# First unit of a two-layer transformer kernel: another order of weight quarters, normed tiles and squares, and the rotary angles computed later

## The chip, the core and the metric

The kernel runs on one core of a Trainium2 chip. Its metric is device time in microseconds (us). The engines meant below are TensorE (PE in the profile, its weight loads PEld), VectorE (DVE), ScalarE (ACT), GpSimd (POOL) and SyncE (SP), which issues the weight loads. Each engine works through its own list of instructions in order; they are tied together by semaphores (`wait_ge`, `then_inc`) that are written by hand.

## The reference

512 tokens of width 1024 go through two layers. Each layer is a feed-forward block, a mixing block (differential attention with rotary angles on queries and keys, beside a gated branch), cross attention to 256 memory rows, and a second feed-forward block:

```
def swiglu(x, wgu, wd):
    gate, up = jnp.split(x @ wgu, 2, axis=-1)
    return (jax.nn.silu(gate) * up) @ wd
cos, sin = rope_tables(positions)
for i in range(2):
    h = h + 0.5 * swiglu(rms_norm(h, ffn1_norm[i]), ffn1_wgu[i], ffn1_wd[i])
    hn = rms_norm(h, mix_norm[i])
    q, k, v, gu, gv = jnp.split(hn @ w_in[i], ...)
    q, k = partial_rope(q, cos, sin), partial_rope(k, cos, sin)
    h = h + concat([diff_attention(q, k, v), gated(gelu(gu), layer_norm(gelu(gv)))]) @ w_out[i]
    h = h + cross_attention(rms_norm(h, ...), rms_norm(mem, ...), ...)
    h = h + 0.5 * swiglu(rms_norm(h, ffn2_norm[i]), ffn2_wgu[i], ffn2_wd[i])
return rms_norm(h, final_norm)
```

## The kernel before

Every product is made of three matmuls of rounded halves: hi by hi, hi by lo, lo by hi. The high half of a weight or an activation is a rounded copy that ScalarE writes (`w_hi`, `hn_hi`); the low half is the difference, which VectorE writes (`w_lo`, `hn_lo`). Weights come in units of 128 x 2048 elements (1 MB) into two slots of `raw`, unit by unit; SyncE issues the loads of a slot once `w_split` says that the low half of the unit two before is done. For each unit, ScalarE rounds (L692), VectorE subtracts (`split_unit`, L1221), TensorE multiplies. A unit of the gate and up weights is 48 matmuls of 512 columns: eight slices k of the contraction, for each a gate and an up product.

The activations are not normed before the product. `hn` is h times the gain; the inverse root mean square of each token is multiplied in afterwards. For the very first block it comes from squares of the input (ScalarE, `square_input`, one instruction for each tile of 128 tokens, each waiting for the one before, L718), a scaling on VectorE (L1297), a power on GpSimd (L603), and four transposes on TensorE that spread it over the partitions (`send_rb`, L2074). ScalarE copies that out as `rb` (L707), and the gating of the first unit starts there.

**The start.** The input comes in four tiles of 128 tokens. TensorE transposes them (L2096) into eight banks; VectorE copies the first six of them to `h`, ScalarE the last two (`copy_input`, L724). The first unit's weights come in four quarters: quarter n has slices 2n and 2n + 1, in two DMAs of 128 KB each (L509). ScalarE writes hi parts in this order: squares of tile 0, the two copies, normed slices 0 and 1, weight quarter 0, slices 2 and 3, quarter 1, slices 4 and 5, squares 1, quarters 2 and 3, slices 6 and 7, squares 2 and 3, then the whole of unit 1. TensorE does the hi products of slices 0 to 3, then their lo-weight products, then waits for the whole low half of the unit (L1292) before slices 4 to 7. After unit 0 it sends `rb`, then starts unit 1.

VectorE, behind the low halves of unit 1, computes the rotary angles (`angles()`, 15 small instructions in a chain, L1310 to L1324) and only then gates unit 0 (L1377).

**The mixing block** starts with the projections GV, QQ, KK, GU, VV, of two units each (48 matmuls a unit, L2053 to L2055). VectorE here splits the two units of QQ, takes statistics of the gated branch (L1767 to L1774), splits the first unit of KK, waits for the inverse deviations that GpSimd raises to a power (L646, `rstd`), norms four tiles with them (L1781 to L1785), writes their low halves (L1789), scales the memory rows (L1795), and then splits the second unit of KK (L1221 again). ScalarE's `late_setup()` takes the sines of the angles after it has rounded the first unit of KK; queries are rotated after the second unit of KK is split.

Of the kernel before, what the change touches and what calls it, by code (L numbers as in the profile page):

```python
# [7 lines left out]
P = 128  # L8
# [5 lines left out]
KT = D // P  # L14
ST = S // P
# [93 lines left out]
def macaron_kernel(nc, x, mem, positions, ffn1_norm, ffn1_wgu, ffn1_wd, mix_norm, w_in,  # L109
# [7 lines left out]
    ACT = mybir.ActivationFunctionType  # L117
# [4 lines left out]
    with ctx:  # L122
        def sem(name):
            return ctx.enter_context(nc.semaphore(name))
# [157 lines left out]
        first_loaded = [sem(f"first_loaded{n}") for n in range(4)]  # L282
        half_split = sem("half_split")
        x_squared = sem("x_squared")
        w_rounded = sem("w_rounded")
        w_split = sem("w_split")
        w_used = sem("w_used")
# [382 lines left out]
        def _(act):  # L670
# [15 lines left out]
            def round_unit(L, u, i=0, per=2):  # L686

                n = unit_no(L, u, i, per)
                s = u % 2
                act.wait_ge(w_loaded[s], 32 * (L * (UNITS // 2) + u // 2 + (per // 2) * i + 1))  # L690
                act.wait_ge(w_used, n + 1)
                act.activation(w_hi[:, s, :], raw[:, s, :], ACT.Copy).then_inc(w_rounded, 1)  # L692

            def round_tile(no, m, gcol):

                act.wait_ge(h_ready, no)
                act.activation(hn_hi[:, slice(m, m + 1), :], h[:, slice(m, m + 1), :], ACT.Copy,
                               scale=gains[:, slice(gcol, gcol + 1)]).then_inc(hn_rounded, 1)
# [10 lines left out]
            def first_unit(n):  # L709
                act.wait_ge(first_loaded[n], 32)  # L710
                act.activation(unit_quarter(w_hi, n), unit_quarter(raw, n), ACT.Copy)\
                   .then_inc((half_rounded, half_rounded, half_rounded, w_rounded)[n], 1)

            def square_input(t):
                act.wait_ge(x_loaded[t], 16)
                if t:
                    act.wait_ge(x_squared, t)
                act.activation(tmp[:, 0:2, :], x_in[:, t, :].rearrange("p (a c) -> p a c", c=S), ACT.Square,  # L718
                               accum_out=xsq[:, t:t + 1]).then_inc(x_squared, 1)

            def copy_input(n):
                t, c = divmod(n, 2)
                act.wait_ge(x_turned, n + 1)
                act.activation(h[:, 4 * c:4 * c + 4, t * P:(t + 1) * P],  # L724
                               ps[:, n % 6, :].rearrange("p (k c) -> p k c", c=P), ACT.Copy).then_inc(h_ready, 1)

            square_input(0)
            copy_input(2 * ST - 2)
            copy_input(2 * ST - 1)
            act.wait_ge(setup_dve, HALF + 1)  # L730
            round_tile(KT, 0, 0)
            round_tile(KT, 1, 1)
            first_unit(0)
            round_tile(KT, 2, 2)
            round_tile(KT, 3, 3)
            first_unit(1)
            round_tile(KT, 4, 4)
            round_tile(KT, 5, 5)
            square_input(1)
            first_unit(2)  # L740
            first_unit(3)
            round_tile(KT, 6, 6)
            round_tile(KT, 7, 7)
            square_input(2)
            square_input(3)
            round_unit(0, 1)
            def late_setup():
                act.wait_ge(lam_sums_ready, 1)
                act.activation(lam_s[:, :, :], lam_s[:, :, :], ACT.Exp).then_inc(setup_act, 1)
                act.wait_ge(angles_ready, 1)  # L750
                for c in range(2):
                    for n in range(2):
                        act.activation(rope[:, :, c, n * HALF:(n + 1) * HALF], ang[:, 2 - c, :, :], ACT.Sin)\
                           .then_inc(setup_act, 1)
# [460 lines left out]
        def _(dve):  # L1215
# [26 lines left out]
            def low_tile(no, m, gcol):  # L1242
                dve.wait_ge(hn_rounded, no)
                dve.scalar_tensor_tensor(out=hn_lo[:, slice(m, m + 1), :], in0=h[:, slice(m, m + 1), :],
                                         scalar=gains[:, slice(gcol, gcol + 1)],
                                         in1=hn_hi[:, slice(m, m + 1), :].bitcast(f32),
                                         op0=ALU.mult, op1=ALU.subtract).then_inc(hn_ready, 1)
# [21 lines left out]
            for n in range(2 * ST - 2):  # L1269
                t, c = divmod(n, 2)  # L1270
                if n == 2:
                    dve.wait_ge(setup_pe, 1)
                    dve.tensor_copy(gains[:, 0:LAYERS * KT], ps[:, 7, 0:LAYERS * KT]).then_inc(setup_dve, 1)
                dve.wait_ge(x_turned, n + 1)
                dve.tensor_copy(h[:, 4 * c:4 * c + 4, t * P:(t + 1) * P],
                                ps[:, n % 6, :].rearrange("p (k c) -> p k c", c=P)).then_inc(h_ready, 1)
            done[0] += 1
            low_tile(1, 0, 0)
            low_tile(2, 1, 1)
# [8 lines left out]
            setup(dve.tensor_copy(gains[:, LAYERS * KT:], ps[:, 6, LAYERS * KT:90]))  # L1288
            low_tile(5, 4, 4)
            low_tile(6, 5, 5)  # L1290
            dve.wait_ge(w_rounded, 1)
            dve.tensor_tensor(out=unit_half(w_lo, 1), in0=unit_half(raw, 1), in1=unit_half(w_hi, 1).bitcast(f32),  # L1292
                              op=ALU.subtract).then_inc(w_split, 1)
            low_tile(7, 6, 6)
            low_tile(8, 7, 7)
            dve.wait_ge(x_squared, ST)
            dve.tensor_scalar(msq[:, :], xsq[:, :], 1.0 / D, EPS, ALU.mult, ALU.add).then_inc(ms_ready, 1)  # L1297
            dve.wait_ge(setup_pe, 3)
# [4 lines left out]
                                        in0=lam_in[:, 2 * n, :].rearrange("p (l d) -> p l d", d=64),  # L1303
                                        in1=lam_in[:, 2 * n + 1, :].rearrange("p (l d) -> p l d", d=64), op=ALU.mult))
            dve.tensor_reduce(lam_s[:, :, :], lam_pr[:, :, :, :], AX.X, ALU.add).then_inc(lam_sums_ready, 1)
            split_unit(0, 1)

            def angles():
                for t in range(ST):
# [8 lines left out]
                for c in (c1, c2, c3):  # L1318
# [4 lines left out]
                setup(dve.tensor_tensor(out=ang[:, 2, :, :], in0=ang[:, 2, :, :], in1=ang[:, 1, :, :], op=ALU.max))  # L1323
                dve.tensor_scalar(ang[:, 2, :, :], ang[:, 2, :, :], -1.0, math.pi / 2, ALU.mult, ALU.add)\  # L1324
                   .then_inc(angles_ready, 1)

            angles()

            def head_gains():
                for l in range(LAYERS):  # L1330
# [418 lines left out]
            for L in range(0, LAYERS):  # L1749
# [10 lines left out]
                split_unit(L, QQ)  # L1760
                mean_square(L * 4 + 2, 7)
                split_unit(L, QQ + 1)
                dve.wait_ge(small_loaded, L * 64 + 64)
                for t in range(ST):
                    dve.wait_ge(gelu_ready, L * 4 + t + 1)
# [284 lines left out]
        def _(pe):  # L2050
# [58 lines left out]
            def ffn(L, f, up, stage):  # L2109
# [5 lines left out]
                def wait_split(kind, i):  # L2115
                    pe.wait_ge(w_split, base + FFN_AT[kind, i] + 3)

                def whole_unit(i, hook=None, waits=False):
                    in_halves = start_of_all and i == 0
                    if in_halves:  # L2120
                        for k in range(4):
                            if k % 2 == 0:
                                pe.wait_ge(half_rounded, k // 2 + 1)
                            pe.wait_ge(hn_ready, hn_no(L, stage, k))
                            for g in range(2):
                                a = g * 1024 + k * P
                                pe.matmul(ps[:, g, :], w_hi[:, 0, a:a + P], hn_hi[:, k, :], start=k == 0, stop=False)
                                pe.matmul(ps[:, g, :], w_hi[:, 0, a:a + P], hn_lo[:, k, :], start=False, stop=False)
                        pe.wait_ge(half_split, 1)
                        for k in range(4):  # L2130
                            for g in range(2):
                                a = g * 1024 + k * P
                                pe.matmul(ps[:, g, :], w_lo[:, 0, a:a + P], hn_hi[:, k, :], start=False, stop=False)
                        pe.wait_ge(setup_dve, HALF + 2)
                        pe.transpose(ps[:, 7, LAYERS * KT:LAYERS * KT + ST], pos_f[:, :], ident[0:ST, 0:ST])\
                          .then_inc(setup_pe, 1)
                    else:
                        wait_split("N", i)
                    for k in range(4 if in_halves else 0, KT):
                        if waits:  # L2140
                            pe.wait_ge(hn_ready, hn_no(L, stage, k))
                        if hook and k in hook:
                            hook[k]()
                        if in_halves and k == 4:
                            wait_split("N", i)
                        for g in range(2):
                            a = g * 1024 + k * P
                            last = product(ps[:, 2 * i + g, :], w_hi[:, i % 2, a:a + P], w_lo[:, i % 2, a:a + P],
                                           hn_hi[:, k, :], hn_lo[:, k, :], k == 0, k == KT - 1)
                    last.then_inc(w_used, 1)  # L2150
# [257 lines left out]
                    token_sums((L * STAGES + stage) * 9, 6)  # L2408

                whole_unit(0, None, True)  # L2410
                if start_of_all:
                    send_rb()
                if not start_of_all:
                    sum_tokens()
                whole_unit(1, None if start_of_all else {4: send_rb}, True)
                whole_unit(2)
                third_unit()
                first_chunk()
# [366 lines left out]
```

## Time and profile before

| | |
|---|---|
| median of 3 runs | 2084.46 us (2083.52 to 2085.33) |
| the profiled execution | 2084.04 us |
| its span | 2082.2 us, 1.8 us less than its time |
| granted TensorE clock | 0.999 over the span |
| DMA | 212.35 MB, 102 GB/s on the mean |

The span is what the profile's clock runs over, from the first instruction to the last. All times "at" a point below count from its start. A line of a timeline gives start, length, engine, source line, operation, what is written and read, and in brackets the idle time ahead of it with what ended it. Where several like instructions follow each other, they are one line with their count, and the length is that of all.

### The profile page before, as it was taken

To read this page: it belongs to the slowest core of one execution; us is meant where nothing else is said; L and a number is where in the kernel's file an instruction comes from. 1 tells how busy PE (TensorE), PEld (TensorE's weight loads), DVE (VectorE), ACT (ScalarE), POOL (GpSimd) and SP (SyncE) were. 2 spreads that over 40 slices of the span, in tenths; PEclk is the share of its full clock that TensorE was granted. 3 is DMA by queue.
4 is the path that set the end of the run, shared out by engine and by line. 5 is a ranking of instruction groups with operands and counts; after the bars stand their busy time and mean duration, and the time that the engine had idled before them with its cause. 6 is when DMAs were issued, how large, how long until landed. Compare 5 with 4: busy or idle time off the path is not lost.

```text
span 2082.2 us, 35834 instructions
## 1 busy us (share of the span) xinstructions
PE 2068.2 (99%) x14719; PEld 1918.0 (92%) x14719; DVE 1654.0 (79%) x2476; ACT 984.8 (47%) x1491; POOL 151.0 (7%) x120
## 2 busy tenths in 40 slices
PE   9999999999999999999999999999999999999998
PEld 7999998889888889999989999988898888999998
DVE  7998886659754789898799988766696458898886
ACT  6444444446533544444464444443564345454443
POOL 0000003100120300000110000030002102000002
PEclk9999999999999999999999999999999999999999
DMA  6333323323331343333233333143233214333321
GB/s 198 102 112 104 101 86 116 122 81 102 101 103 41 91 127 112 115 104 92 72 121 112 112 107 112 59 149 102 68 116 101 81 61 132 102 112 92 112 87 57
DMA packets 268031, 212.35 MB, mean 102 GB/s; under 512 B 7422, under 2 KB 234332, under 8 KB 267868
## 3 DMA queue, kind: packets, MB, share of 16 engines
q1 hardware_dynamic: 264608, 205.55, 31.7%
q10 hardware_dynamic: 3260, 4.51, 0.7%
q8 instruction: 117, 1.92, 0.4%
q14 instruction: 46, 0.38, 0.1%
HBM read 207.93 MB, written 2.10 MB: 101 GB/s over the span
## 4 chain that ended last, share of the span: by engine, by line
PE 92%; DVE 5%; ACT 2%; issue 1%; DMA 0%; POOL 0%; SPq 0%; DVEq 0%; ACTq 0%; POOLq 0%
PE ps L2180 18%; PE ps L2053 13%; PE ps L2055 13%; PE ps L2054 13%; PE ps L2360 11%; PE ps L2361 11%; PE ps L2362 11%; DVE nb L1909 1%; DVE w_lo L1231 1%; ACT ex L1120 1%; DVE ex L1929 1%; DVE ps L1907 0%; PE ps L2514 0%; PE ps L2705 0%; DMA x_in<-in_x_dram 0%
## 5 line engine op out<-in xcount | busy, mean ns | idle before, releaser
L2180 PE MATMUL ps<-hid_hi,wn_hi 128*128 128x256 f32 x1088 | 211.9, 276 | 0.0
L2180 PE MATMUL ps<-hid_lo,wn_hi 128*128 128x256 f32 x1088 | 211.9, 276 | 0.0
L2180 PE MATMUL ps<-hid_hi,wn_lo 128*128 128x256 f32 x1088 | 211.8, 276 | 0.0
L1490 DVE SCALAR_TENSOR_TENSOR h<-ps,h 128x512 f32<-128x512 f32 x224 | 152.6, 683 | 30.4 <-PE ps L2180 26.8
L692 ACT ACTIVATE w_hi<-raw 128x2048 fp32r<-128x2048 f32 x61 | 117.0, 1918 | 123.1 <-PE ps L2055 90.8
L2180 PEld LDWEIGHTS ps<-hid_lo,wn_hi 128*128 128x128 f32 x1088 | 163.8, 188 | 0.0
L2180 PEld LDWEIGHTS ps<-hid_hi,wn_hi 128*128 128x128 f32 x1088 | 163.8, 188 | 0.0
L2180 PEld LDWEIGHTS ps<-hid_hi,wn_lo 128*128 128x128 f32 x1088 | 163.7, 188 | 0.0
L2360 PE MATMUL ps<-hn_hi,form_hi 128*128 128x256 f32 x576 | 159.0, 276 | 0.0
L2362 PE MATMUL ps<-hn_hi,form_lo 128*128 128x256 f32 x576 | 159.0, 276 | 0.0
L2361 PE MATMUL ps<-hn_lo,form_hi 128*128 128x256 f32 x576 | 159.0, 276 | 0.0
L2360 PE MATMUL ps<-t_hi,form_hi 128*128 128x256 f32 x576 | 159.0, 276 | 0.0
L2361 PE MATMUL ps<-t_lo,form_hi 128*128 128x256 f32 x576 | 159.0, 276 | 0.0
L2362 PE MATMUL ps<-t_hi,form_lo 128*128 128x256 f32 x576 | 159.0, 276 | 0.0
L2360 PE MATMUL ps<-t_hi,more_hi 128*128 128x256 f32 x576 | 159.0, 276 | 0.0
L2361 PE MATMUL ps<-t_lo,more_hi 128*128 128x256 f32 x576 | 159.0, 276 | 0.0
L2362 PE MATMUL ps<-t_hi,more_lo 128*128 128x256 f32 x576 | 159.0, 276 | 0.0
L1221 DVE TENSOR_TENSOR w_lo<-raw,w_hi 128x2048 fp32r<-128x2048 f32 x49 | 114.3, 2332 | 48.6 <-ACT w_hi L692 48.3
L2053 PE MATMUL ps<-hn_hi,w_hi 128*128 128x512 f32 x376 | 147.8, 393 | 0.7 <-DVE w_lo L1292 0.5
L2055 PE MATMUL ps<-hn_hi,w_lo 128*128 128x512 f32 x376 | 146.5, 390 | 0.0
L2054 PE MATMUL ps<-hn_lo,w_hi 128*128 128x512 f32 x376 | 146.4, 389 | 0.0
L598 POOL TENSOR_TENSOR sumsq<-sumsq,tmp 128x512 f32<-128x512 f32 x56 | 102.0, 1821 | 340.4 <-ACT tmp L703 335.5
(356 smaller groups left out, 6161.8 us busy)
## 6 DMA issues: line engine op xcount, KB each, us to landing
sraw<-in_ffn_wgu_dram SPq DMA_DIRECT2D x144, 512.0 KB, 4.9
raw<-in_ffn_wd_dram SPq DMA_DIRECT2D x48, 512.0 KB, 3.8
raw<-in_ffn_wd_dram SPq DMA_DIRECT2D x80, 256.0 KB, 4.0
raw<-in_w_in_dram SPq DMA_DIRECT2D x40, 512.0 KB, 4.5
raw<-in_cross_wkv_dram SPq DMA_DIRECT2D x32, 512.0 KB, 4.2
raw<-in_ffn_wgu_dram SPq DMA_DIRECT2D x30, 512.0 KB, 4.8
raw<-in_w_out_dram SPq DMA_DIRECT2D x16, 512.0 KB, 4.3
raw<-in_cross_wq_dram SPq DMA_DIRECT2D x16, 512.0 KB, 3.9
```

The lines of the kernel that those rows point to most:

```text
L598: pool.tensor_tensor(out=sumsq[:, :], in0=sumsq[:, :], in1=tmp[:, m2, :], op=ALU.add)\
L692: act.activation(w_hi[:, s, :], raw[:, s, :], ACT.Copy).then_inc(w_rounded, 1)
L1120: last = act.activation(ex[:, b, br, 0:N], ps[:, 4 + 2 * b + br, 0:N], ACT.Exp, bias=nb[:, b, br:br + 1], accum_out=sm[:, b, br:br + 1])
L1221: dve.tensor_tensor(out=w_lo[:, s, 0:z], in0=raw[:, s, 0:z], in1=w_hi[:, s, 0:z].bitcast(f32), op=ALU.subtract).then_inc(w_split, 1)
L1490: dve.scalar_tensor_tensor(out=h[:, m, :], in0=ps[:, down_bank(c, m), :], scalar=0.5, in1=h[:, m, :], op0=ALU.mult, op1=ALU.add).then_inc( ...
L2053: pe.matmul(dst, a_hi, b_hi, start=start, stop=False)
L2054: pe.matmul(dst, a_hi, b_lo, start=False, stop=False)
L2055: return pe.matmul(dst, a_lo, b_hi, start=False, stop=stop)
L2180: last = pe.matmul(ps[:, bank, c], w, src[:, b, c], start=opens, stop=stop and n == 2, skip_group_check=half == 1)
L2360: pe.matmul(dst, a_hi, b_hi, start=start and k == 0, stop=False, skip_group_check=not start)
L2361: pe.matmul(dst, a_hi, b_lo, start=False, stop=False, skip_group_check=not start)
L2362: last = pe.matmul(dst, a_lo, b_hi, start=False, stop=k == 3, skip_group_check=not start)
```

## The change

ScalarE's order at the start becomes: squares 0, the copy of the seventh bank only (under a semaphore of its own, `last_left`), slice 0, quarter 0, slices 1 and 2, quarter 1, slices 3 and 4, quarter 2, slice 5, quarter 3, slices 6 and 7, unit 1, and then squares 1 to 3. The eighth bank is copied by VectorE. Slices 0 to 3 no longer wait for it.

TensorE does the hi products of slices 4 to 7 as soon as the weights are rounded, and their lo-weight products last. `send_rb` moves from the front of unit 1 to between its slices 1 and 2. VectorE splits unit 1 ahead of the mean squares and the small set-up work. `angles()` moves into the mixing block of layer 0, between the split of the second unit of QQ and the statistics.

```
 ScalarE
             square_input(0)
-            copy_input(2 * ST - 2)
-            copy_input(2 * ST - 1)
+            copy_last_left()
             act.wait_ge(setup_dve, HALF + 1)
-            round_tile(KT, 0, 0)
-            round_tile(KT, 1, 1)
+            act.wait_ge(last_left, 1)
+            round_tile(KT - 2, 0, 0)
             first_unit(0)
-            round_tile(KT, 2, 2)
-            round_tile(KT, 3, 3)
+            round_tile(KT - 2, 1, 1)
+            round_tile(KT - 2, 2, 2)
             first_unit(1)
+            round_tile(KT - 2, 3, 3)
             round_tile(KT, 4, 4)
+            first_unit(2)
             round_tile(KT, 5, 5)
-            square_input(1)
-            first_unit(2)
             first_unit(3)
             round_tile(KT, 6, 6)
             round_tile(KT, 7, 7)
-            square_input(2)
-            square_input(3)
             round_unit(0, 1)
+            for t in range(1, ST):
+                square_input(t)
 VectorE
+            dve.wait_ge(x_turned, 2 * ST)
+            dve.tensor_copy(h[:, 4:8, (ST - 1) * P:ST * P],
+                            ps[:, (2 * ST - 1) % 6, :]...).then_inc(h_ready, 2)
...
+            low_tile(7, 6, 6)
+            low_tile(8, 7, 7)
             dve.wait_ge(w_rounded, 1)
             dve.tensor_tensor(out=unit_half(w_lo, 1), ...).then_inc(w_split, 1)
-            low_tile(7, 6, 6)
-            low_tile(8, 7, 7)
+            split_unit(0, 1)
             dve.wait_ge(x_squared, ST)
...
-            split_unit(0, 1)
...
-            angles()
...
                 split_unit(L, QQ + 1)
+                if L == 0:
+                    angles()
 TensorE, unit 0, behind the products of slices 0 to 3
+                        pe.wait_ge(w_rounded, 1)
+                        for k in range(4, KT):   # w_hi by hn_hi and w_hi by hn_lo
...
                         wait_split("N", i)
+                        for k in range(4, KT):   # w_lo by hn_hi
...
-                if start_of_all:
-                    send_rb()
-                whole_unit(1, None if start_of_all else {4: send_rb}, True)
+                whole_unit(1, {2 if start_of_all else 4: send_rb}, True)
```

## Rows read from the trace of the kernel before

**Rows 1.** The page, part 1: engine, busy us, share of span, instructions.
```profile
PE 2068.2 (99%) x14719; PEld 1918.0 (92%) x14719; DVE 1654.0 (79%) x2476; ACT 984.8 (47%) x1491; POOL 151.0 (7%) x120
```
**Rows 2.** Waits of TensorE: us in total, times, longest us.
```profile
PE ps L2127 <- ACT w_hi L711: 0.9, 1, 0.9
PE ps L2053 <- DVE w_lo L1292: 0.5, 1, 0.5
```
**Rows 3.** Timeline of ScalarE at the start.
```profile
9.31 1.09 ACT L724 ACTIVATE h<-ps 128x512 f32<-128x512 f32 x2
10.50 1.33 ACT L697 ACTIVATE hn_hi<-h,gains 128x512 fp32r<-128x512 f32 x2
11.74 0.61 ACT L711 ACTIVATE w_hi<-raw 128x512 fp32r<-128x512 f32 x1
...
19.77 1.06 ACT L718 ACTIVATE tmp<-x_in 128x1024 f32<-128x1024 f32 x1
20.83 1.90 ACT L692 ACTIVATE w_hi<-raw 128x2048 fp32r<-128x2048 f32 x1
```
**Rows 4.** Second and tenth weight DMA: issue (timeline), landing (DMA view, us from issue).
```profile
3.44 0.49 SPq L509 DMA_DIRECT2D raw<-in_ffn_wgu_dram  x1
raw<-in_ffn_wgu_dram SPq DMA_DIRECT2D x1, 128.0 KB, 7.8
...
9.78 3.52 SPq L500 DMA_DIRECT2D raw<-in_ffn_wgu_dram  x1
raw<-in_ffn_wgu_dram SPq DMA_DIRECT2D x1, 512.0 KB, 9.5
```
**Rows 5.** Timelines of VectorE and GpSimd at the start.
```profile
11.25 1.41 DVE L1244 SCALAR_TENSOR_TENSOR hn_lo<-h,gains,hn_hi 128x512 fp32r<-128x512 f32 x2 [1.69 <-ACT hn_hi L697]
...
22.76 2.29 DVE L1221 TENSOR_TENSOR w_lo<-raw,w_hi 128x2048 fp32r<-128x2048 f32 x1 [0.43 <-ACT w_hi L692]
...
21.21 1.02 POOL L603 TENSOR_TENSOR rtok<-msq,m_half 128x4 f32<-128x4 f32 x1 [19.19 <-DVE msq L1297]
```
**Rows 6.** Timeline of TensorE at the start.
```profile
12.40 0.50 PE L2127 MATMUL ps<-hn_hi,w_hi 128*128 128x512 f32 x1 [0.86 <-ACT w_hi L711]
...
24.34 0.60 PE L2074 MATMUL ps<-ident,rtok 128*128 128x128 f32 x4
...
25.11 0.50 PE L2053 MATMUL ps<-hn_hi,w_hi 128*128 128x512 f32 x1 [0.17 <-DVE w_lo L1221]
```
**Rows 7.** Timeline of VectorE: first of the angles, and what follows the last.
```profile
24.97 1.02 DVE L1310 TENSOR_SCALAR ang<-invf,pos_t 128x8 f32<-128x8 f32 x4
...
28.10 0.68 DVE L1377 TENSOR_TENSOR Gn<-ps,rb 128x512 f32<-128x512 f32 x1
```
**Rows 8.** Timelines of TensorE, GpSimd and VectorE in layer 0's mixing block.
```profile
394.09 0.39 PE L2053 MATMUL ps<-w_hi,hn_hi 128*128 128x512 f32 x1
404.97 0.39 PE L2053 MATMUL ps<-w_hi,hn_hi 128*128 128x512 f32 x1
...
382.49 2.90 POOL L646 TENSOR_TENSOR rstd<-vareps,m_half 128x16 f32<-128x16 f32 x1 [4.95 <-DVE vareps L1774]
...
385.42 2.29 DVE L1221 TENSOR_TENSOR w_lo<-raw,w_hi 128x2048 fp32r<-128x2048 f32 x1 [2.94 <-ACT w_hi L692]
387.62 1.11 DVE L1781 TENSOR_SCALAR k_tok<-k_tok,mv,rstd 128x128 f32<-128x128 f32 x4
...
401.28 2.28 DVE L1221 TENSOR_TENSOR w_lo<-raw,w_hi 128x2048 fp32r<-128x2048 f32 x1
```
**Rows 9.** Timelines of VectorE and GpSimd later in layer 0: a power beside a subtraction.
```profile
716.78 1.22 DVE L1358 TENSOR_TENSOR t_lo<-t_raw,t_hi 128x1024 fp32r<-128x1024 f32 x1
716.95 1.93 POOL L603 TENSOR_TENSOR rtok<-msq,m_half 128x4 f32<-128x4 f32 x1 [3.13 <-DVE msq L1251]
```
**Rows 10.** Timelines of VectorE and TensorE: first tile of the blocked stage.
```profile
72.32 0.42 DVE L1402 TENSOR_TENSOR G<-ps,G 128x256 f32<-128x256 f32 x1 [0.41 <-ACT G L835]
...
73.06 0.28 PE L2360 MATMUL ps<-t_hi,form_hi 128*128 128x256 f32 x1
```

More of the change, by code:

```diff
@@ L284, in macaron_kernel @@
         x_squared = sem("x_squared")
+        last_left = sem("last_left")
         w_rounded = sem("w_rounded")
@@ L719, in square_input, with copy_last_left @@
                                accum_out=xsq[:, t:t + 1]).then_inc(x_squared, 1)
-            def copy_input(n):
-                t, c = divmod(n, 2)
+            def copy_last_left():
+                n = 2 * ST - 2
                 act.wait_ge(x_turned, n + 1)
-                act.activation(h[:, 4 * c:4 * c + 4, t * P:(t + 1) * P],
-                               ps[:, n % 6, :].rearrange("p (k c) -> p k c", c=P), ACT.Copy).then_inc(h_ready, 1)
+                act.activation(h[:, 0:4, (ST - 1) * P:ST * P], ps[:, n % 6, :].rearrange("p (k c) -> p k c", c=P), ACT.Copy)\
+                   .then_inc(last_left, 1)
             square_input(0)
-            copy_input(2 * ST - 2)
-            copy_input(2 * ST - 1)
+            copy_last_left()
             act.wait_ge(setup_dve, HALF + 1)
-            round_tile(KT, 0, 0)
-            round_tile(KT, 1, 1)
+            act.wait_ge(last_left, 1)
+            round_tile(KT - 2, 0, 0)
             first_unit(0)
-            round_tile(KT, 2, 2)
-            round_tile(KT, 3, 3)
+            round_tile(KT - 2, 1, 1)
+            round_tile(KT - 2, 2, 2)
             first_unit(1)
+            round_tile(KT - 2, 3, 3)
             round_tile(KT, 4, 4)
+            first_unit(2)
             round_tile(KT, 5, 5)
-            square_input(1)
-            first_unit(2)
             first_unit(3)
@@ L1276, in _ @@
                                 ps[:, n % 6, :].rearrange("p (k c) -> p k c", c=P)).then_inc(h_ready, 1)
+            dve.wait_ge(x_turned, 2 * ST)
+            dve.tensor_copy(h[:, 4:8, (ST - 1) * P:ST * P],
+                            ps[:, (2 * ST - 1) % 6, :].rearrange("p (k c) -> p k c", c=P)).then_inc(h_ready, 2)
             done[0] += 1
@@ L2136, in whole_unit @@
                           .then_inc(setup_pe, 1)
-                    else:
-                        wait_split("N", i)
-                    for k in range(4 if in_halves else 0, KT):
+                        pe.wait_ge(w_rounded, 1)
+                        for k in range(4, KT):
+                            pe.wait_ge(hn_ready, hn_no(L, stage, k))
+                            for g in range(2):
+                                a = g * 1024 + k * P
+                                pe.matmul(ps[:, g, :], w_hi[:, 0, a:a + P], hn_hi[:, k, :], start=False, stop=False)
+                                pe.matmul(ps[:, g, :], w_hi[:, 0, a:a + P], hn_lo[:, k, :], start=False, stop=False)
+                        wait_split("N", i)
+                        for k in range(4, KT):
+                            for g in range(2):
+                                a = g * 1024 + k * P
+                                last = pe.matmul(ps[:, g, :], w_lo[:, 0, a:a + P], hn_hi[:, k, :],
+                                                 start=False, stop=k == KT - 1)
+                        last.then_inc(w_used, 1)
+                        return
+                    wait_split("N", i)
+                    for k in range(KT):
                         if waits:
@@ L2143, in whole_unit @@
                             hook[k]()
-                        if in_halves and k == 4:
-                            wait_split("N", i)
                         for g in range(2):
```

## Prediction

> **What bounds the kernel now.** I read the page's busy shares first: TensorE is busy for 99% of the span, VectorE for 79%, ScalarE for 47% [rows 1]. So time can come only from TensorE's idle stretches, and none of its work is removed. Next the waits of TensorE: at the start two long ones are named, 0.9 us for the first rounded weights and 0.5 us for the second low half [rows 2]. Then the timelines: the real work starts at 12.40 and unit 1 at 25.11, with four transposes between the units [rows 6]. Later TensorE meets hardly a wait; what counts there is how much room each low half has, which the timeline shows and the table of waits does not.
>
> **The start, step by step.** A unit of 48 matmuls takes 404.97 - 394.09 = 10.88 us [rows 8], 0.227 each.
>
> *ScalarE.* Two copies took 1.09, so one takes about 0.55 and ends at 9.86. The normed slice then starts at 9.96 instead of 10.50 and takes about 0.62 (10.50 to 11.74 for two) [rows 3]. Quarter 0 would be next at 10.6, but its second DMA, issued at 3.44, lands 7.8 later, at 11.24 [rows 4]. Rounding it (0.61) ends at 11.89, where before it ended at 12.35: TensorE starts 0.45 earlier, not the 1.1 that the order alone would give. Slices and quarters follow, 0.52 to 0.62 each, the last slice ends near 18.3. Unit 1 can't be rounded before its second load lands, at 9.78 + 9.5 = 19.28 [rows 4]; 1.90 for it gives 21.2, where before it ended at 22.73 [rows 3]. The three squares, 1.22 apart as each waits for the one before, start near 21.1, 22.3, 23.5. Before, the last square started at 19.77 and the power ended at 21.21 + 1.02 = 22.23, 2.46 later [rows 3, 5]; so it now ends at 26.0.
>
> *VectorE.* The eighth copy fits into its idle 1.69 [rows 5] and costs nothing; if that cover were gone, 0.6. A low slice takes 0.7. The low half of slices 0 and 1 is late now: slice 1 is rounded behind quarter 0 and is ready at 13.25. Slice 3 follows at 15.0, half of the first low weights (half of 2.29, about 1.2) at 16.2, the other slices at 0.7 each until 19.2, the second half at 20.3. Unit 1 is split from 21.2 to 23.5, where before it ended at 25.05 [rows 5].
>
> *TensorE.* From 11.93: 48 matmuls (10.88), 0.1 for one small transpose, 0.4 of waiting for slice 1, 0.1 for the half, 0.2 for two restarts. Sum 23.6; unit 1 starts there, just behind its low half at 23.5. Slices 0 and 1 of it (12 matmuls) end at 26.35, the power has ended at 26.0, so the spreading transposes don't wait. They take 0.65. Unit 1 therefore ends 25.11 - (23.65 + 0.65) = 0.8 earlier than before.
>
> *What the head start keeps.* `rb` arrives some 2.1 later than before (27.05 for 24.94 [rows 6]). The angles, 28.10 - 24.97 = 3.13 us [rows 7], no longer stand ahead of the first gating, so this starts at 27.7 instead of 28.10; but the table load for the silu, behind `rb` on ScalarE, makes the silu some 0.15 late, and with it the loads and VectorE's work up to the blocked stage. There VectorE waited 0.41 for ScalarE and gave `G` at 72.74, 0.3 ahead of TensorE at 73.06 [rows 10]. With TensorE 0.8 early and VectorE's queue 0.15 late, that `G` comes at 72.4 against 72.26: 0.2 of the head start goes. I take -0.6, with -0.9 and +0.2 as ends (the lower if nothing of it is lost, the upper if the wait for slice 1 and the late queue cost 0.4 each more).
>
> **The angles in their new place.** They are 3.13 us of VectorE [rows 7] in front of the statistics. Behind them in its queue stand the statistics, the split of KK's first unit, the norming, the memory rows and the split of KK's second unit, for which TensorE comes at 404.97. This split ended at 401.28 + 2.28 = 403.56: 1.4 of room [rows 8].
>
> First the plain count. The power for `rstd` started at 382.49 and took 2.90 [rows 8], then VectorE still waited for ScalarE and split KK's first unit; norming started at 387.62. Shifted by 3.13 the power would run 385.62 to 388.52, norming would start at 388.6, 1.0 late, and 0.4 of the room would be left. Cost nothing.
>
> But the shift puts the power beside the split. The split needs `w_hi` (ready at 385.4) and follows the statistics at once, at about 385.5; the power starts 0.1 behind it. The trace has the same constellation: a subtraction from SBUF started at 716.78 and took 1.22, a power started at 716.95, and took 1.93 [rows 9], where a power of the same shape otherwise takes 1.02 [rows 5]. It ended 0.88 behind the end of the subtraction, as if 0.14 of it had run before and the rest had waited; the subtraction was not longer. So here: the split ends at 385.52 + 2.29 = 387.8, the power 2.90 - 0.14 later, at 390.6; norming starts at 390.6, 3.0 late, and the split of KK's second unit runs 404.3 to 406.6. TensorE waits 1.6, and a restart costs 0.1 more: +1.7. The ends are 0 (the plain count) and +2.2 (a power stretched in the ratio 1.93 to 1.02 takes 5.5 and ends at 391.1).
>
> The Trainium skill, "SBUF — State Buffer", section "Who interferes with whom", says that a VectorE instruction with two SBUF inputs and a GpSimd instruction that reads SBUF exclude each other for their whole length, and that the one which comes second stands still. By that rule the sum is +1.7 whichever of the two is first, since both must have run before the norming; by the ratio it would be +2.2. The row agrees with the rule (end of the subtraction plus 0.88), but shows it only for a power of 4 elements, not of 16.
>
> The next split in VectorE's queue is that of GU, which TensorE needs a whole unit (10.88) later, so nothing of the delay is passed on; without that cover up to 3.0 would come again. ScalarE's sines wait for angles that are done before the statistics, and so before 385.4, when ScalarE asks. Layer 1 has no angles and isn't changed.
>
> **Sum.** -0.6 + 1.7 = +1.1 us on the profiled execution's 2084.04, which is 0.4 below the median shown. On the median: 2084.46 + 1.1 = 2085.5.
>
> **Rivals.**
>
> A. The power isn't held up, or holds up little: the room of 1.4 covers the plain 1.0. Only the start counts: -0.6, 2083.9. For it: rows 9 show another shape, and the order at 385.5 hangs on 0.1 us. Against it: in either order the two would have to run side by side.
>
> B. Slower on the other side of my sum: unit 1's load decides the squares. Rounding of unit 1 now stands ahead of three squares and has no room behind the landing at 19.28, where it had 1.5 before (20.83) [rows 3, 4]. The place is `send_rb` in the middle of unit 1, the price is each microsecond that the power ends later than 26.35, and it decides from a landing 0.4 later than in this trace. With a landing 1.9 later it costs 1.5, beside 1.7 in the mixing block and hardly any gain kept: +2.8, 2087.2. For it: single loads here take between 7.8 and 9.5 to land. Against it: the loads are issued as before, so they should land as before.
>
> C. The start does what its order promises, the stall is as forecast, and the sum is near zero: gain 1.1 or more if landings come earlier, 2084.8. It is inside the range.
>
> A bigger gain is excluded: all waits of TensorE at the start are below 2 us together [rows 2, 6].
>
> **Chances.** Forecast 0.6, A 0.2, B 0.1, C 0.1. What a measurement of this kernel can tell from no change is 0.2%, 4.2 us, and all four cases lie within it; outside of it I leave 0.02 for faster and 0.04 for slower (an unseen stall that comes back in each blocked stage). The range, 2083.1 to 2087.0, holds A, the forecast and C with half a microsecond of scatter, and most of B.
>
> **What would show it.** TensorE's first matmul of unit 0 at 11.9 and of unit 1 at 23.6; unit 1 rounded from 19.3; the first power ended at 26.0 and no wait before the spreading transposes; a wait of 0.2 for `G` near 72.3. In the mixing block, L646 of layer 0 some 5.0 long instead of 2.90 and a wait of TensorE for L1221 of 1.6 near 404, while layer 1 keeps 2.90 and no wait. If L646 is 2.90 and the wait is missing, A is right; if TensorE waits ahead of L2074, B.

## The result, and the profile after

| | time, median | executions | ratio to before |
|---|---|---|---|
| before | 2084.39 us (2083.44 to 2085.49) | 20 | |
| after | 2087.69 us (2085.80 to 2090.83) | 20 | 1.0017, 95% interval 1.0011 to 1.0024 |

The changed kernel is 3.3 us slower, three times the forecast's +1.1 and 0.7 above the upper end of the range. It stays within the 0.2% that was named as the bound of "same". Its executions also scatter twice as much: 5.0 us from lowest to highest, against 2.05. The profiled execution took 2087.64 (span 2085.9), 3.60 above that of before.

The same line of the page's part 1 as in [rows 1]: TensorE is busy 2.4 us longer, though it does no more matmuls.

```profile
PE 2070.6 (99%) x14719; PEld 1919.2 (92%) x14719; DVE 1655.8 (79%) x2477; ACT 984.4 (47%) x1490; POOL 152.7 (7%) x120
```

The waits of TensorE. The two of [rows 2] are gone, a wait for the low half of the second unit of key weights (KK) is new:

```profile
PE ps L2056 <- DVE w_lo L1221: 1.9, 1, 1.9
...
PE ps L2099 <- DMA x_in<-in_x_dram: 0.6, 1, 0.6
PE ps L2195 <- issue: 0.3, 1, 0.3
```

**Where the time came from.** I compared the start of TensorE's nth matmul in both traces (14719 in each); the difference, after minus before, is called the shift here. It reads -0.35 at 30 us, once `rb` is sent, +0.33 at 75 us, +0.45 from 80 to 404 us, +4.19 at 412 us, +3.68 at the end. So the head start is small, it is lost with the first blocked tile, and 3.74 us come in at one place of the mixing block.

*The start*: ScalarE (answers to [rows 3]), then the spreading transposes, `G`'s product on VectorE and TensorE behind it (to [rows 6, 10]).

```profile
16.21 0.63 ACT L712 ACTIVATE w_hi<-raw 128x512 fp32r<-128x512 f32 x1 [1.30 <-DMA raw<-in_ffn_wgu_dram]
19.98 1.92 ACT L693 ACTIVATE w_hi<-raw 128x2048 fp32r<-128x2048 f32 x1 [0.78 <-DMA raw<-in_ffn_wgu_dram]
24.27 1.06 ACT L719 ACTIVATE tmp<-x_in 128x1024 f32<-128x1024 f32 x1
27.77 0.60 ACT L708 ACTIVATE rb<-ps 128x512 f32<-128x512 f32 x1 [2.35 <-PE ps L2077]
28.39 1.28 ACT L784 ACT_TABLE_LOAD   x1
29.68 0.63 ACT L784 ACTIVATE Gn<-Gn 128x512 f32<-128x512 f32 x1
...
27.14 0.60 PE L2077 MATMUL ps<-ident,rtok 128*128 128x128 f32 x4
...
72.79 0.41 DVE L1403 TENSOR_TENSOR G<-ps,G 128x256 f32<-128x256 f32 x1
...
73.31 0.36 PE L2375 MATMUL ps<-t_hi,form_hi 128*128 128x256 f32 x1
```

ScalarE now waits for two loads where the old order had room. TensorE's first product is a different matter: it did not wait for weights in this execution. The first quarter was rounded at 11.94. Ahead of the product stand 16 transposes of the identity whose results nobody reads (`keep_busy`), behind the turning of the last input tile, and these ended at 12.24. Three rows of after, then that of before, where they ended at 11.54:

```profile
11.32 0.62 ACT L712 ACTIVATE w_hi<-raw 128x512 fp32r<-128x512 f32 x1
...
10.33 1.91 PE L2084 MATMUL ps<-ident 128*128 128x128 f32 x16
12.35 0.47 PE L2130 MATMUL ps<-hn_hi,w_hi 128*128 128x512 f32 x1
...
9.63 1.91 PE L2081 MATMUL ps<-ident 128*128 128x128 f32 x16
```

The spreading transposes at 27.14 did not wait for the power, but the silu stands behind `rb` (27.77 to 28.37) and the table load: it starts at 29.68. Its row of before:

```profile
28.82 0.63 ACT L784 ACTIVATE Gn<-Gn 128x512 f32<-128x512 f32 x1 [1.94 <-DVE Gn L1377]
```

So it is 0.86 late, where 0.15 was forecast. `G` at 72.79 is 0.47 later than in [rows 10] (0.86 less the 0.41 for which VectorE had waited there).

*The mixing block* (answers to [rows 7] and [rows 8]): VectorE and GpSimd, and the first product that waited.

```profile
377.40 1.41 DVE L1313 TENSOR_SCALAR ang<-invf,pos_t 128x8 f32<-128x8 f32 x4
...
386.35 2.29 DVE L1221 TENSOR_TENSOR w_lo<-raw,w_hi 128x2048 fp32r<-128x2048 f32 x1
...
386.46 4.93 POOL L647 TENSOR_TENSOR rstd<-vareps,m_half 128x16 f32<-128x16 f32 x1 [8.48 <-DVE vareps L1777]
...
405.09 2.28 DVE L1221 TENSOR_TENSOR w_lo<-raw,w_hi 128x2048 fp32r<-128x2048 f32 x1
...
407.43 0.50 PE L2056 MATMUL ps<-w_hi,hn_hi 128*128 128x512 f32 x1 [1.85 <-DVE w_lo L1221]
```

The angles run from 377.40 to 380.92, 3.52 and not 3.13 us. The power is 4.93 long beside the split (forecast 5.0), and the split for which TensorE waits ends at 407.37 (forecast 406.6).

*The clock.* What no step of the prediction had stands in the stretches behind the wait. Columns: stretch, its length, busy time of each engine, then the granted clock of TensorE (1.00 is its level of 2.4 GHz, 0.50 that of 1.2 GHz), DMA share and GB/s.

```profile
405.00:407.50 2.50, 0.65 (x4) 0.23 (x2) 2.50 (x4) 2.50 (x4) 0.00 (x0) 1.00 0.00 0
409.00:412.00 3.00, 3.00 (x8) 2.32 (x8) 2.83 (x10) 0.00 (x0) 0.00 (x0) 0.50 0.96 327
```

The first stretch holds the idle time; in the second TensorE is never idle, yet eight matmuls fall into it where an execution at full clock has fifteen (e9, below). Three of them:

```profile
409.14 0.63 PE L2056 MATMUL ps<-w_hi,hn_hi 128*128 128x512 f32 x1
409.57 0.63 PE L2057 MATMUL ps<-w_lo,hn_hi 128*128 128x512 f32 x1
410.00 0.63 PE L2058 MATMUL ps<-w_hi,hn_lo 128*128 128x512 f32 x1
```

They are 0.43 apart instead of 0.227. Of the 3.74 that come in, 2.02 are there at the first product behind the wait, 1.72 come behind it.

### The profile page after: what moved, and what is told of

Same layout as the page of the kernel before. It is cut to its first block, busy times and chain, and to the rows that moved or that the text cites. A ratio compares the mean times of both kernels' runs of the same rounds, so it can differ in the third digit from the quotient of the medians.

```text
span 2085.9 us, 35836 instructions
## 1 busy us (share of the span) xinstructions
PE 2070.6 (99%) x14719; PEld 1919.2 (92%) x14719; DVE 1655.8 (79%) x2477; ACT 984.4 (47%) x1490; POOL 152.7 (7%) x120
## 4 chain that ended last, share of the span: by engine, by line
PE 91%; DVE 6%; ACT 1%; issue 1%; DMA 0%; SPq 0%; POOL 0%; DVEq 0%; ACTq 0%; POOLq 0%
PE ps L2195 18%; PE ps L2056 13%; PE ps L2058 13%; PE ps L2057 13%; PE ps L2375 11%; PE ps L2376 11%; PE ps L2377 11%; DVE nb L1912 1%; DVE w_lo L1231 1%; ACT ex L1120 1%; DVE ex L1932 1%; DMA raw<-in_ffn_wgu_dram 0%; DVE ps L1910 0%; PE ps L2718 0%; PE ps L2527 0%
```

## The experiments

Theory at the outset: the angles stall TensorE in the mixing block by 2 us and the clock falls behind the stall (+1.6 in some executions); the start gains nothing, because `rb`, and behind it VectorE, is late. Rival: the start, through its landings, makes the excess and the scatter. The kernel before was run on the same chip as each group. A ratio's 95% interval is about 1.9 us to either side in all of these groups, so among kernels that lie 1 to 2 us apart the traces decide, not the medians.

**Each half alone** (before: 2084.37, 33 executions).

```
e1: the kernel before, angles() moved ahead of layer 0's statistics
e2: the changed kernel, angles() back at their old place
```

> The kernel before with one edit: the angles stand behind the split of QQ's second unit, the start stays as it was. Theory M (the slowdown sits in the mixing block: the power is held up by the split, TensorE waits about 2.0 us for KK's second unit, and the granted clock then halves for about 3.4 us, which costs about 1.7 more): +3.3 to +3.9 us, L647's counterpart near 4.9 long, one wait of 1.8 to 2.0 for the split, one stretch at half clock. Rival S (the new order of the start costs the time, the angles add only the wait): +1.7 to +2.0, and the rest is missing here.

Measured: 2086.21 (2085.83 to 2088.22), ratio 1.0011 (1.0002 to 1.0019). In its profile the start's shift is -0.14, TensorE waits 1.9 for `w_lo`, and the shift goes from -0.11 to +3.68, with the half clock in it. The median, +1.8, is what the rival expected and misses the theory's +3.3; the profiled execution, +3.1, comes near the theory. So the wait came as forecast, but the fall of the clock is no fixed part of it.

> The changed kernel with the angles back in their old place, behind the small set-up work and ahead of the first gating. Theory M: no wait in the mixing block and no stretch at half clock there; what is left is the start: the power is 4 us later than before, the angles push the first gating to about 30, and TensorE loses about 1.4 us at the first blocked tile, so +0.5 to +1.5. Rival S: +1.5 to +2 or more, with the loss spread over the start.

Measured: 2084.68 (2084.37 to 2086.12), ratio 1.0003 (0.9994 to 1.0012); no wait for `w_lo`. Its first product came at 11.61, its head start is -1.09 at 30 us, and +0.93 at 150 us: 2 us go in the first blocked stage, as here the angles too stand ahead of the first gating.

**Three ways round the stall** (e3 and e4 on the chip of e1; e5 on that of e9).

```
e3: angles() behind mss, ahead of the split of KK's first unit
e4: KK's second unit does its 32 products with w_hi first, then those with w_lo
```

> The changed kernel with the angles two instructions further back in VectorE's queue: behind the variances and the mean squares of the memory, ahead of the split of KK's first unit, so beside the power, where VectorE waited 2.9 us for ScalarE. Theory M: the power takes 2.9 to 3.3, norming starts no more than 0.5 late, no wait for KK's second unit, clock full: +0.4 (the start alone), within -0.3 and +1. Rival P (any VectorE work beside the power holds it up): the power takes over 4, but as the split no longer stands behind both, at most 1 us is lost and the 1.4 of room covers it: the same time, told apart only by the length of L647. Rival S: +1.5 to +2.

Measured: 2084.68 (2083.91 to 2086.83), ratio 1.0003 (0.9995 to 1.0012). The angles fill VectorE's idle time beside the power, which is back at its old length:

```profile
383.18 1.03 DVE L1313 TENSOR_SCALAR ang<-invf,pos_t 128x8 f32<-128x8 f32 x4
...
386.31 2.28 DVE L1221 TENSOR_TENSOR w_lo<-raw,w_hi 128x2048 fp32r<-128x2048 f32 x1
388.52 1.11 DVE L1784 TENSOR_SCALAR k_tok<-k_tok,mv,rstd 128x128 f32<-128x128 f32 x4
...
383.29 2.90 POOL L647 TENSOR_TENSOR rstd<-vareps,m_half 128x16 f32<-128x16 f32 x1 [4.95 <-DVE vareps L1775]
```

> The changed kernel with its angles where they are; only TensorE's second unit of KK is reordered: its 32 products with the rounded weights run first and wait only for ScalarE's rounding, its 16 products with the low weights last, behind the wait for the split. Theory M: the power still takes 4.9 and VectorE is just as late, but TensorE has 7.3 us of work in front of that wait: no idle time, full clock, +0.4 (within -0.3 and +1). If VectorE's lateness costs in another place too, +1 to +2 and a wait behind KK.

Measured: 2085.04 (2083.69 to 2085.54), ratio 1.0003 (0.9994 to 1.0012). The power stays long, but TensorE has work until `w_lo` is there; no wait, clock full:

```profile
387.47 4.94 POOL L647 TENSOR_TENSOR rstd<-vareps,m_half 128x16 f32<-128x16 f32 x1 [8.47 <-DVE vareps L1777]
```

They stand 0.3 and 0.7 above the kernel before. The changed kernel itself was not run in this group; in three others it stands 3.3, 4.2 and 3.7 above. The stall with what follows it is most of the loss, and two different edits that take it away show it.

```
e5: in layer 0 split_unit(L, KK) behind the first norm tile, so that nothing
    runs beside the power
```

> The changed kernel with the split of KK's first unit of layer 0 behind the norming of the first tile instead of ahead of it, so that VectorE stands still beside the power. If the split holds the power up, L647 takes 2.90 again in layer 0 and norming starts 2.0 earlier, but the split's 2.2 comes out of it again ahead of KK's second unit: the wait there stays about 2.0 and the time +2.3 to +4. If the power is slow for another reason (the time at which it runs), it takes 4.9 here too and the wait grows to 4.

One profiled execution, 2086.30 (before on this chip 2083.95): the power is 2.90 again, and TensorE waits no less.

```profile
386.20 2.90 POOL L647 TENSOR_TENSOR rstd<-vareps,m_half 128x16 f32<-128x16 f32 x1 [8.48 <-DVE vareps L1777]
...
391.62 2.29 DVE L1221 TENSOR_TENSOR w_lo<-raw,w_hi 128x2048 fp32r<-128x2048 f32 x1
...
404.99 2.29 DVE L1221 TENSOR_TENSOR w_lo<-raw,w_hi 128x2048 fp32r<-128x2048 f32 x1
...
407.34 0.50 PE L2059 MATMUL ps<-w_hi,hn_hi 128*128 128x512 f32 x1 [2.03 <-DVE w_lo L1221]
```

The stretched power is therefore no loss of its own: power and split have to run one after the other between the statistics and the rest of the norming, in whichever order. What costs is 3.5 us of VectorE ahead of both, while VectorE stands idle beside the power.

**Is it the idle time that makes the clock fall?** (before: 2083.95, 27 executions.)

```
e9: the changed kernel again
e6: the changed kernel, and ahead of KK's second unit in layer 0
    for _ in range(8): pe.matmul(ps[:, bank, :], nil[:, :], hn_hi[:, 0, :], ...)
```

> The changed kernel itself again, as the measure for the next one on the same chip. Start +0.3 to +0.7 (from the runs with the angles elsewhere), wait for KK's second unit +2.0, and in a part of the executions +1.7 for a stretch at half clock: each time lies near 2086.8 or near 2088.5, the median between, +2.4 to +4.1. If the clock has nothing to do with it, the times lie in one group.

Measured: 2088.13 (2086.37 to 2090.57), ratio 1.0019 (1.0010 to 1.0028). The eleven times don't fall into two groups; they are spread over the whole range, so the clock is not all that scatters. In its profile the same wait of 1.9 leaves the clock full:

```profile
409.00:412.00 3.00, 3.00 (x15) 2.49 (x14) 2.76 (x15) 0.00 (x0) 0.00 (x0) 1.00 0.84 264
```

> The changed kernel, with 8 matmuls of 512 columns put in front of TensorE's wait for KK's second unit in layer 0; their stationary tile is all zeros and they add nothing to the sums. They take 1.8 of the 2.0 us of idle time. If idle time is what brings the clock down, it stays full in every execution and the time is that of the wait and the start alone, +2.3 to +2.7, with no second group above: 0.5 to 1.5 below the changed kernel's median. If the clock falls for another reason, or the wait alone is the cost, it is no faster than the changed kernel, +3.3.

Measured: 2087.41 (2085.52 to 2088.24), ratio 1.0016 (1.0007 to 1.0025). The filler takes the place of the wait, to the tenth of a microsecond:

```profile
405.80 1.97 PE L2468 MATMUL ps<-hn_hi,nil 128*128 128x512 f32 x8
407.82 0.50 PE L2059 MATMUL ps<-w_hi,hn_hi 128*128 128x512 f32 x1
```

The median falls by 0.7 and the spread from 4.2 to 2.7 us; all 11 executions have a mean clock of 0.999 or 1.000, where 4 of 11 of e9 have 0.998. This speaks for the theory, weakly: the median missed the +2.3 to +2.7 that were expected, and a listed 0.998 is no sure sign of a fall behind a wait. The kernel before has it in 5 of 33 executions on each of two chips and in none of 27 here. And 3.5 us stay with no listed drop in them.

**Does the start keep its gain if `rb` comes earlier?**

```
e8: e3, and square 1 ahead of the third quarter, square 2 ahead of unit 1,
    send_rb at step 1 of unit 1 instead of 2
e7: the same with the angles where the change has them
```

> The changed kernel with the angles beside the power (as in the earlier run), squares 1 ahead of weight quarter 2 and squares 2 ahead of unit 1, where ScalarE waited 1.3 and 0.8 us for loads, and the spreading transposes between slices 0 and 1 of unit 1. The power then ends about 1.5 earlier, `rb` and the first gating with it, and VectorE is no longer late at the first blocked tile: the head start of 0.2 to 1.1 at unit 2 isn't lost there, so 0.8 below the kernel with the angles beside the power and -0.3 to -0.8 against before. If the head start goes in another place, +0.3 as with the angles moved alone.

Measured (chip of e9): 2083.74 (2082.84 to 2084.76), ratio 0.9998 (0.9989 to 1.0007). The shift is +0.25 at 30 us and still +0.25 at 150 us: nothing is lost in the blocked tiles. The silu starts 0.11 later than before, on TensorE that is 0.25 late, and VectorE waits for ScalarE again ahead of `G`:

```profile
28.93 0.63 ACT L785 ACTIVATE Gn<-Gn 128x512 f32<-128x512 f32 x1
...
72.57 0.42 DVE L1404 TENSOR_TENSOR G<-ps,G 128x256 f32<-128x256 f32 x1 [0.45 <-ACT G L836]
```

It is the lowest of all versions, 0.2 below the kernel before where 0.3 to 0.8 were expected, and cannot be told from it.

**Do the parts add up?** By the medians so far, 0.3 (e2) and 1.8 (e1) stand against 3.3 to 4.2. So all were run side by side (before: 2085.50, 33 executions), e10 as e2, e11 as e1, e12 the changed kernel.

> The changed kernel with the angles back behind the second feed-forward block, as in e2 (first unit new, angles old), beside e11 and e12 on one chip. Parts that add up: the first unit's new order is worth the same wherever it stands, +0.3 to +1.5 against the kernel before on this chip, and its profile has a shift at 80 us between 0 and 1.5 (in the seven profiles with the new first unit so far: 0.05 to 1.47, mean 0.76), set by when the weight quarters and unit 1's weights land. Rival (the two parts make each other worse): +0.3 here as before, and the changed kernel more than 1.0 above this one and e11 taken together. A clock below 0.999 in about one execution in ten, as in the kernel before (5 of 33, 0 of 27).

> The kernel before with the angles alone moved, as in e1. Expected +1.8 to +2.4: the stall of 2.0 at the first product with w_lo of the key unit, and in some executions the clock at half for some microseconds behind it (those have a mean clock of 0.998 and stand 1.3 to 2.5 above the others). Its start is that of the kernel before, so its full-clock executions should spread no more than 1.5 us.

> The changed kernel once more, on the chip of e10 and e11. Parts that add up: its difference from the kernel before is that of e10 plus that of e11 within 0.7, with the spread of both (4 us from lowest to highest). Parts that make each other worse: more than 1.0 above the sum (batches one and two, on two chips, gave 0.3 + 1.8 against 3.3 to 4.2). If executions with clock 0.998 are left out, the drop goes and what is left over the sum is the first unit's alone.

> The changed kernel with squares 1 and 2 back in ScalarE's gaps (square 1 before the third weight quarter's rounding, square 2 before unit 1's) and the spreading of rms one step earlier; the angles where the change has them. Stall as in the changed kernel (2.0). If what is lost at the start is ScalarE's three squares standing behind unit 1's rounding, and through them VectorE late in the first blocked tile, this is 0.6 to 1.2 below e12. If it is the landing of the quarters, which no order of the squares changes, it is within 0.3 of e12.

| kernel | median | range | over before |
|---|---|---|---|
| e10, start alone | 2085.52 | 2084.59 to 2087.89 | 0.0 |
| e11, angles alone | 2087.06 | 2086.57 to 2089.11 | +1.6 |
| e12, changed | 2089.20 | 2087.19 to 2091.37 | +3.7 |
| e7, changed, `rb` earlier | 2088.19 | 2085.42 to 2090.17 | +2.7 |

The ratios are 1.0000 (0.9992 to 1.0009), 1.0011 (1.0002 to 1.0020), 1.0017 (1.0008 to 1.0026) and 1.0011 (1.0002 to 1.0020). The parts do not add up by their medians, 1.6 against 3.7, and both fell short of what was expected of them (+0.3 and +1.8 at the least). e7's median is 1.0 lower than e12's, and its shift is 1.18 at 30 us and 1.18 at 150 us, where e12 goes from 1.03 to 1.93. The traces show that this 0.9 is the late `rb`; the medians agree, but could not show it alone. e11, with the old start, had a shift of 1.64 at 30 us: there the weights came late under the old order too (ScalarE waited 0.8 for the first quarter, TensorE's first product came at 13.85).

**More executions of the changed kernel in profile**, e13 to e15, and one of e6, e16 (before, one execution: 2083.64).

> The changed kernel, one profiled execution more. (a) The clock falls behind the wait for w_lo: matmuls at 0.43 apart for some 3 us, +1.6 there, start shift at 80 us 0 to 1. (b) Clock full, start shift above 1. (c) The wait above 2.3. Seen so far in three executions: wait 1.9 in each, clock fallen in one, start shift 0.45, 1.01 and 1.53.

> As e13. If (a), two or three of the executions e13 to e15 have the clock at half behind the wait; if the chance is that of the angles alone (3 of 22 executions with a mean clock of 0.998), none or one.

> As e13. The executed time of each of the three is, by the terms read so far, that of the kernel before on this chip plus 0.0 to 1.2 of the start, 2.0 of the wait and 0 or 1.6 of the clock; a time more than 0.5 above the terms read in its own trace would mean a fourth cause.

> The changed kernel with eight matmuls that add zeros ahead of the wait, one execution more. Clock full throughout; wait and filler together 2.0 to 2.2 by the first product behind them. If its shift over the kernel before is above 2.8 at the end, it must be the start's (b), since neither (a) nor a longer idle is left.

The six profiled executions of the changed kernel. The second column is the time less that of before on its chip (the median; for e13 to e15 the one execution); the others are read from the shifts.

| execution | over before | shift at 30 us | at 150 us | added at the first product behind the wait | added behind it |
|---|---|---|---|---|---|
| after | +3.25 | -0.35 | +0.45 | 2.02 | 1.72 |
| e9 | +3.55 | +0.40 | +1.38 | 2.02 | 0.12 |
| e12 | +2.66 | +1.03 | +1.93 | 2.03 | 0.14 |
| e13 | +4.47 | -0.15 | +0.95 | 2.03 | 1.75 |
| e14 | +5.16 | -0.02 | +1.33 | 2.02 | 1.74 |
| e15 | +3.75 | +0.70 | +1.27 | 2.03 | 0.17 |

The wait is the same in all. Behind it 0.12 to 0.17 come at full clock, 1.72 to 1.75 where the clock is at half, in three of six: the half clock costs 1.6. e14's stretches:

```profile
405.00:407.50 2.50, 1.37 (x7) 0.79 (x5) 2.50 (x3) 2.50 (x5) 0.00 (x0) 1.00 0.00 0
...
409.00:412.00 3.00, 3.00 (x9) 2.33 (x8) 2.78 (x13) 0.00 (x0) 0.00 (x0) 0.50 0.89 280
```

Its mean clock is listed as 0.999, so the listed means do not find all falls, and counts by them are too low. The third explanation, a longer wait in unseen executions, has nothing for it in six traces. e16 took 2086.64, 3.0 over before, with a full clock, a shift of +0.63 at 150 us and 2.17 at the filled wait; what it lies above the kernel before is these two.

**When the clock fell.** Ten profiled executions have an unfilled wait: the six of the table, e1, e5, e7 and e11. Count from the moment at which the granted clock first rises in the span (5.2 to 8.2 us). In the four where it fell again, the wait began 399.7 to 400.5 us after that moment, and the fall came 402.8 after it in each. In the six others the wait began at 398.3 to 399.0, or at 401.1 to 401.4. The waits are equally long; what differs is when they come. By the same count e6's filler began at 400.0, where it could keep the clock up, but e16's at 399.3, outside of the stretch in which the clock ever fell, so of the two traces with the filler only e6 bears on its use. No run moved the wait on purpose.

**What stays open.** The mean of the six is 3.8 over before. Start (mean 1.2 at 150 us), wait (2.15) and half of 1.6 make 4.2; some 0.3 is given back between 1000 and 1400 us. That closes for the changed kernel. It does not for the medians of its parts: the new start alone has +0.93 and +1.19 at 150 us in its two profiles, yet its median is only 0.0 to 0.3 above before, and the filled kernel's median, 3.5 over before, lies above both of its profiled executions (+2.5 and +3.0). The trace of before is one execution of a kernel whose times themselves vary by 2 us, so some of "shift at 150 us" belongs to that one execution: the three traces with the old start have 0, -0.14 (e1) and +1.64 (e11) there. Between the sum of the parts and the whole 1.2 to 2.1 us by the medians are not explained.

## Why the prediction was wrong, by its steps

**TensorE's first matmul at 11.93, a head start of 0.8.** This step failed. The first matmul came at 12.35 in the profile after, and between 11.40 and 13.75 in the other five. ScalarE was on time (first quarter rounded at 11.94, forecast 11.89). What the sum left out is TensorE's own queue: the 16 transposes stand ahead of the product and ended at 12.24 where they had ended at 11.54, since the last input tile came later. They decide in this execution and in e14; in the other four TensorE waited for the first quarter, because ScalarE had waited 1.1 to 1.5 us for its load. The forecast took one execution's landings as fixed. The head start was 0.35 here, and on the mean of the six there was none (+0.27 at 30 us).

**Squares and power.** Right in kind: the power ended at 26.73 (forecast 26.0, with unit 1 rounded 0.7 later than forecast), and TensorE did not wait ahead of L2077 in any trace. So rival B's condition came true, a landing over 0.4 later, but not its price: TensorE itself came to the transposes only at 27.14.

**"VectorE's queue 0.15 late, 0.2 of the head start goes".** This step failed too. The queue was 0.86 late. It hung on TensorE and not on the power: ScalarE waited 2.35 for the transposes, which began at 27.14 instead of 26.35, because unit 1 began at 24.28 instead of 23.65. What goes behind unit 1 is 0.80 in this execution and 0.57 to 1.35 in the six. Measured against its own TensorE, the silu is 1.2 later than in the kernel before (0.86 + 0.35), where the forecast's numbers imply 0.95 (0.15 + 0.8) and rows 10 left 0.7 of room; and the loss goes on in the tiles behind the first. e7 and e8 show the cause: with `rb` one step earlier it vanishes. In place of -0.6 the start is worth +0.45 in this execution and +1.2 on average, against the one trace of before; by the medians of the start alone it is 0.0 to 0.3. ("All waits of TensorE at the start are below 2 us together" also leaves out the 2.1 us for `mask` ahead of its first transposes, which the change doesn't touch.)

**The angles, 3.13 us.** 3.52: the four products with the positions took 1.41 beside a GpSimd instruction where they took 1.02 in [rows 7]. The norming started 3.8 late, 0.45 of which is the start's, so 3.4 instead of 3.0.

**Power held up by the split, wait of TensorE.** Right in kind, and nearly in size: 4.93 for 5.0, a cost of 2.14 (2.02 and 0.12) for 1.7; the 0.4 are those of the angles. The Trainium skill, "SBUF — State Buffer", section "Who interferes with whom", has a VectorE instruction with two SBUF inputs and a GpSimd instruction that reads SBUF exclude each other; the trace agrees, now for 16 elements as well (the power ended 0.14 short of 2.90 behind the end of the split at 388.64). e5 adds what the prediction already used: either order costs the same. Layer 1 kept its power and had no wait.

**Sum +1.1, nothing else.** The last failed step, and in this execution the largest, is one that is missing: the wait was priced as 1.6 of idle time and 0.1 of restart. In half of the profiled executions TensorE then ran at its lower level, 1.60 more, almost as much as the wait itself. That is what carried the profiled execution from about +2 to +3.6, and it is part of the scatter. The range's upper end came from rivals that had no such term; with it, a stall of 2 us should have been given as 2.1 to 3.8.

## What to carry to other kernels

Price an idle stretch of TensorE in two parts, the wait and the matmuls behind it at the lower clock, and give the second as a chance. Before work is moved to another place in a queue, look for the idle stretch next to it: 3.5 us of angles cost 2 to 4 us ahead of the statistics and nothing that can be told beside the power, a few lines further down. And a head start of half a microsecond that is read from the landings of one execution is no forecast: the first product came at 12.27 to 13.85 in three traces with the old order and at 11.40 to 13.75 in six of the changed kernel.

## What the runs showed of the hardware

- The clock can fall after 1.9 us without matmuls. It fell in 4 of the 10 profiled executions with such a wait (three of the changed kernel, e1) and stayed full in the others (e9, e12, e15, e5, e7, e11). With the filler in place of the wait it stayed full in both profiled executions. In the four that fell, the wait began 399.7 to 400.5 us after the clock's first rise in the span; in the six others it began earlier (up to 399.0) or later (from 401.1). Behind the wait the granted clock stood at 0.50 up to about 412 us of the span, and this cost 1.6 us.
- The four TENSOR_SCALAR of the angles (8 columns each, from 377.40) took 1.41 us where they began beside an affine select of GpSimd, the row below of the profile after, and 1.03 beside the power of 16 elements (e3). All of the difference is in the first of the four, 0.61 us for 0.22.

```profile
376.11 1.87 POOL L643 TENSOR_SCALAR_AFFINE_SELECT wsr<-wsr 128x512 f32<-128x512 f32 x1 [2.04 <-DMA bs_b<-in_gmlp_bs_dram]
```
